# Scores of a gated-linear-attention head: four full-width products replaced by ten 32 by 32 blocks

## What is computed

```python
bcum = jnp.cumsum(lg, axis=3)
q_dec = q * jnp.exp(bcum)
k_intra = k * jnp.exp(-bcum)
causal = jnp.tril(jnp.ones((C, C), bool))
att = jnp.where(causal, jnp.einsum('nbhid,nbhjd->nbhij', q_dec, k_intra), 0.0)
o_intra = jnp.einsum('nbhij,nbhje->nbhie', att, v)
```

## Time and profile before

| what | value |
|---|---|
| median of 3 runs | 1655.56 us (1652.19, 1655.56, 1656.39) |
| profiled execution, span | 1651.1 us |
| time that the page gives around that span | none; the three runs lie 1.1 to 5.3 us above it |
| TensorE busy | 1613.4 us, 98% |
| VectorE, ScalarE, GpSimd busy | 818.7, 458.2, 375.8 us |
| mean granted TensorE clock | 0.99 |

### The profile page before, as it was taken

How to read it: one execution, slowest core, us unless ns; L and a number is a source line. 1 busy time by engine, 2 the same in 40 slices (tenths; PEclk the granted TensorE clock), 3 DMA queues, 4 the chain that set the end, 5 groups by cost and what they waited for, 6 DMA issues and landing times.

```text
span 1651.1 us, 25118 instructions
## 1 busy us (share of the span) xinstructions
PE 1613.4 (98%) x9827; PEld 1501.1 (91%) x9827; DVE 818.7 (50%) x1271; ACT 458.2 (28%) x969; POOL 375.8 (23%) x384
## 2 busy tenths in 40 slices
PE   6999999999999999998999999999999999999996
PEld 5899999999999999998788898888998989979896
DVE  4654449443944475457224562245622356224475
ACT  4321112111211121123325413154040541315423
POOL 3022212211211212211314223133130322314310
PEclk8999999999999999998999999999999999999998
DMA  9512221221122121210202212022120221201312
GB/s 330 193 56 87 62 63 42 84 74 42 55 78 64 57 67 54 77 41 27 64 18 73 84 40 77 13 64 84 53 66 12 64 96 40 77 13 40 110 37 108
DMA packets 137545, 115.03 MB, mean 70 GB/s; under 512 B 6013, under 2 KB 120281, under 8 KB 137442
## 3 DMA queue, kind: packets, MB, share of 16 engines
q1 hardware_dynamic: 135616, 112.87, 22.0%
q10 hardware_dynamic: 1834, 0.74, 0.2%
HBM read 99.05 MB, written 15.00 MB: 69 GB/s over the span
## 4 chain that ended last, share of the span: by engine, by line
PE 94%; DVE 3%; SPq 1%; DMA 1%; ACT 1%; issue 0%; ACTq 0%; DVEq 0%
PE psA L549 40%; PE psB L549 29%; PE psB L1804 8%; PE psA L1804 4%; PE psB L1860 2%; PE psB L1877 2%; PE psX L1842 2%; PE psB L1868 2%; PE psX L1897 1%; DVE a_hi L637 1%; PE psB L1909 1%; PE psX L1720 1%; DMA ada<-in_ada_w 1%; DVE y_rows L1606 0%; PE psB L1910 0%; PE psX L1661 0%
## 5 line engine op out<-in xcount | busy, mean ns | idle before, releaser
L344 POOL TENSOR_TENSOR w_lo<-stage,w_hi 128x1024 fp32r<-128x1024 f32 x100 | 249.7, 2496 | 891.1 <-ACT w_hi L339 891.1
L339 ACT ACTIVATE w_hi<-stage 128x1024 fp32r<-128x1024 f32 x100 | 107.0, 1070 | 433.7 <-PE psB L549 297.6
L549 PE MATMUL psA<-h_hi,w_hi 128*128 128x362 f32 (+1 forms) x864 | 210.9, 349 | 4.1 <-DVE h_lo L453 3.8
L549 PE MATMUL psA<-h_lo,w_hi 128*128 128x362 f32 (+1 forms) x864 | 193.6, 329 | 0.0
L549 PE MATMUL psA<-h_hi,w_lo 128*128 128x362 f32 (+1 forms) x864 | 193.1, 329 | 0.0
L549 PEld LDWEIGHTS psA<-h_hi,w_hi 128*128 128x128 f32 x864 | 151.4, 190 | 27.1 <-issue 21.2
L549 PEld LDWEIGHTS psA<-h_hi,w_lo 128*128 128x128 f32 x864 | 151.5, 190 | 0.0
L549 PEld LDWEIGHTS psA<-h_lo,w_hi 128*128 128x128 f32 x864 | 151.4, 190 | 0.0
L549 PE MATMUL psA<-a_hi,w_hi 128*128 128x362 f32 (+1 forms) x480 | 109.7, 334 | 2.6 <-DVE a_lo L640 1.9
L549 PE MATMUL psB<-h_hi,w_hi 128*128 128x362 f32 (+1 forms) x480 | 109.7, 331 | 0.0
L549 PE MATMUL psB<-h_hi,w_lo 128*128 128x362 f32 (+1 forms) x480 | 107.9, 327 | 0.0
(11 more groups left out here) (345 smaller groups left out, 2790.6 us busy)
## 6 DMA issues: line engine op xcount, KB each, us to landing
stage<-in_gla_w_in SPq DMA_DIRECT2D x40, 512.0 KB, 3.8
stage<-in_pool_w_in SPq DMA_DIRECT2D x32, 512.0 KB, 4.1
ada_stage<-in_ada_w SPq DMA_DIRECT2D x24, 512.0 KB, 3.8
ada<-in_ada_w SPq DMA_DIRECT2D x16, 512.0 KB, 8.4
stage<-in_pool_w_out SPq DMA_DIRECT2D x16, 512.0 KB, 3.4
v<-in_state_gla SPq DMA_DIRECT2D x32, 256.0 KB, 2.6
out_new_gla_sample<-v SPq DMA_DIRECT2D x32, 256.0 KB, 2.1
stage<-in_gla_w_out SPq DMA_DIRECT2D x16, 512.0 KB, 3.7
```

Of the source, the lines that this page charges most:

```text
L339: nc.scalar.activation(slot_hi(plan, j), stage[:, j % 2, :], ACT.Copy).then_inc(lay.hi_done, 1)
L344: nc.gpsimd.tensor_tensor(slot_lo(plan, j), stage[:, j % 2, :], slot_hi(plan, j).bitcast(f32), ALU.subtract).then_inc(lay.lo_done, 1)
L549: last = nc.tensor.matmul(ps[u][:, t, 0:width], weight(w[:, p, :], k), a[:, k, n0:n0 + width], start=(k == 0 and pas == 0), stop=(k == kt ...
```

## The change

`scores` no longer makes one matmul of 128 keys by 32 queries for each query block. It makes ten, each of 32 keys by 32 queries, and each into the 32 partitions of `psX` that belong to its keys, that is into the group of 32 columns of the array with the same number. The order is by distance of key block and query block: first the four with distance 0 (column groups 0, 1, 2, 3), then three with distance 1 (groups 0, 1, 2), two with distance 2 (0, 1), one with distance 3 (group 0). The six blocks that the mask drops are not written; the mask keeps their old content out of `att`. The zeroing of `Kp` and the semaphore `kp_zero` are gone.

```diff
                 wait_apart(pool, L1.unit_done, units(GP, g, GP.unit["LG"] + 1))
-                pool.memset(Kp[:], 0.0).then_inc(kp_zero, 1)
...
                 nc.scalar.activation(ks_s[:], ks_s[:], ACT.Exp).then_inc(smp_exp, 1)
-                act.wait_ge(kp_zero, g + 1)
...
-                    for b in range(4):
-                        last = nc.tensor.matmul(X[0][:, b * CH:(b + 1) * CH], Kp[:, b, :], qd[:, b * CH:(b + 1) * CH],
-                                                start=True, stop=True)
+                    for back in range(4):
+                        for b in range(back, 4):
+                            keys = slice((b - back) * CH, (b - back + 1) * CH)
+                            last = nc.tensor.matmul(X[0][keys, b * CH:(b + 1) * CH], Kp[:, b, keys],
+                                                    qd[:, b * CH:(b + 1) * CH], start=True, stop=True)
                     last.then_inc(att_done, 1)
```

More of the change, by code:

```diff
@@ L286, in trunk @@
         dec_ready = sem("dec_ready")
-        kp_zero, kp_exp, kp_ready = sem("kp_zero"), sem("kp_exp"), sem("kp_ready")
+        kp_exp, kp_ready = sem("kp_exp"), sem("kp_ready")
         qd_arg, qd_exp, qd_ready = sem("qd_arg"), sem("qd_exp"), sem("qd_ready")
```

## The result

The changed kernel takes 1644.40 us in the median of 4 runs (1641.99 to 1645.86) against 1654.99 for the kernel before (1652.19 to 1656.39): ratio 0.9937, 95% interval 0.9923 to 0.9950. That is 10.6 us less where 7.5 were forecast. The profiled spans differ by 9.5 us, 1651.1 to 1641.6.

The account below looks back on a forecast made before the run. TensorE's stream was taken as the bound: 0.25 + 0.03 + 0.22 + 0.12 + 0.11 = 0.73 against 0.97 us per chunk, 7.7 us over 32 chunks, less 0.2 for waits, gives 1648 us. Range 1644.5 to 1655 us.

Parts of the forecast that it names:

- What bounds the kernel: TensorE, busy 98% of the span: the end moves with the length of its own stream.
- TensorE's idle share: Sign: it should rise slightly, since drains show as idle, though the span falls.
- The zeroing is worth nothing: Dropping four `Kp` zeroings of 0.52 us on POOL gains nothing, as ACT's other wait covers them.
- Entry, 0.25: Change from full width to 32-column groups: 0.25 us from last filling matmul to first scores load.
- The body: Ten scores blocks in four column groups side by side: eighth record 0.22 us after the first, 0.031 a round.
- Exit, 0.12: After the last scores matmul, 0.03 us of stream and 0.09 of emptying before the transpose's load.
- the 0.03 for an open first load: The first 32-column scores load lies open for 0.03 us, a quarter of 0.11.
- Then the load of the transpose, 128 columns, lies open for 0.11, which it does not now.: Behind the scores, the transpose's load newly costs 0.11 us per chunk.
- Who must keep up: POOL's last `Kp` slice in chunk 2 is tightest: about 0.09 us left, at most 0.05 charged per head.
- a wait for `Kp` in chunk 2: Sign: if TensorE waits for this buffer there, the prediction is wrong.
- The round that does not halve again: Rival: scores rounds stay near 0.06 us, gain 1.3 us, 1654 us; chance 0.17.
- The case that does not run side by side: Rival: scores records go one after another, 19 steps, 1660 us, or 1677 at 0.06 a step; chance 0.09.

Follow-up runs that it names:

- e1: The changed kernel with the zeroing of `Kp` on GpSimd and ACT's wait for it put back: 1644.56 us, ratio 0.9943 to the kernel before.
- e5: The changed kernel with work left out, one matmul of 32 keys by 32 queries in column group 0 per chunk: 1636.60 us, one run.
- e3: The changed kernel with all 16 blocks of 32 by 32, also those the mask drops, and the zeroing back: 1643.67 us, one run.
- e4: The changed kernel with scores in 64-column halves, six matmuls of 64 keys by 32 queries, zeroing back: 1649.30 us, ratio 0.9977 to the kernel before.
- e2: The changed kernel with the same ten blocks ordered by key block, so that neighbours share a column group: 1645.66 us, one run.
- e7: The changed kernel with the transpose of the keys' rows ahead of the scores instead of behind: 1643.75 us, ratio 0.9938 to the kernel before.
- e6: The changed kernel with work left out, one full-width matmul of 128 keys by 32 queries per chunk, zeroing back: 1634.95 us, one run.
- e8: The changed kernel with the samples' 32-column products moved directly behind the scores at three of four places per head: 1642.48 us, ratio 0.9930.

## Why the prediction came out as it did

*What bounds the kernel.* Right: TensorE's own stream was shortened and the end moved with it. One sign named for it did not come: TensorE's idle share did not rise (1651.1 - 1613.4 = 37.7 us before, 1641.6 - 1604.7 = 36.9 after, 2.28% and 2.25%). The gaps show on the row of the loads instead.

*The zeroing is worth nothing.* Right (e1).

*Entry, 0.25.* Right to the digit, in the trace after and in e5. The Trainium skill's rule in TensorEngine Tiling (Array Packing), Key Properties, that a change of tiling mode drains TensorE, agrees: 28 gaps of 0.23 us, and 0.15 us lost by a lone narrow product against a wide one.

*The body.* Right: 0.24, in the listed window, though the sum had 0.22. The fullest group sets the length (e3), and a round at 64 columns is nearly twice that at 32 (0.058 against 0.032, e4). That the order of the blocks would not matter was nowhere claimed, and it does (e2).

*Exit, 0.12.* Right: the transpose's load came at 0.62 as summed. That this sum is exact is partly luck: the 0.03 for an open first load is not there (the first scores matmul is recorded 0.002 us behind its load), and the body is 0.02 longer than its term.

*"Then the load of the transpose, 128 columns, lies open for 0.11, which it does not now."* This is the step that failed; it is why the gain per chunk was put at 0.24 and not at 0.33. From the last scores matmul to L1860, in the single records of chunk 1, it was 0.255 us before and is 0.293 after, 0.04 more, where the forecast let the tail grow by 0.12 (0.12 + 0.11 in place of 0.11). In the kernel before that load is issued at 857.24 but takes 0.22, where the same load takes 0.139 in the changed kernel and 0.143 in e7. The 0.08 between them is waiting behind the last load of the scores: it too began only when the scores' loads had ended, and lay as open as it does now. The starts say the same. At chunk 1 of the kernel before these are the last three loads of the scores and the load of the transpose:

```profile
862.41 0.41 PEld L1842 LDWEIGHTS psX<-qd,Kp 128*128 128x128 f32 x3
862.66 0.22 PEld L1852 LDWEIGHTS psB<-ident,ks 128*128 128x128 f32 x1
```

Three loads of 0.19 that start 0.11 apart fill the 0.41, so the last starts at 862.63; the next one's turn would be 0.11 later, and the transpose's is recorded 0.03 later, again 0.08 ahead of its turn.

Two like points are the load's real begin, 857.24 + 0.08 = 857.32 before, 0.94 after the last filling matmul at 856.38, against 0.62 now: 0.32 a chunk; or L1860 in both, 0.33. I had set an end that includes the transpose's load (0.73) against one where its matmul was merely issued (0.97). Over 32 chunks the difference is 0.09 x 32 = 2.9 us, the whole of the gap between 7.5 and 10.4. What the runs show is the length of the load and the cost of e7; that the 0.08 is a wait in the queue of loads is read from these lengths and starts and not measured by itself.

*Who must keep up.* Right in place and in the size charged: in chunk 2 of each head the keys' buffer came last, 0.05 us late (at most 0.05 charged). But a wait for `Kp` in chunk 2 stood among the signs that the prediction is wrong, and it came. The working had left 0.09 us of slack with a gain of 0.24; with the 0.33 that TensorE really gained, 0.08 + 0.25 - 0.33 leaves nothing. So this sign follows from the same step, the charge for the transpose's load. e5 and e6 show how near the next bound is: with the chunk made shorter by another 0.2 us it is 0.22 late with an entry to hide under.

*The rivals.* The round that does not halve again is refuted by the 0.24 and by e4. The Trainium skill's rule in TensorE: Matmul & The Clock Gate, Part 3, that a load overlaps a running matmul only when the row group differs, is contradicted with it: all ten blocks use all rows, and 20 loads with 20 matmuls start within 0.24 us. The case that does not run side by side is refuted as well; with a bad order a third of it comes true (e2). One sum in it was off: slower by 0.3%, which is 5 us or 0.156 a chunk, begins at (0.22 + 0.24 + 0.156) / 19 = 0.032 a step and not at 0.034; no chance hangs on it.

## What to carry to other kernels

A group of small products that is bound by its weight loads gains from narrow column groups when the fullest group's rounds, plus one entry and one exit (here 0.24, 0.25 and 0.12 us), are less than the wide loads (0.86); one lone product loses by it, and products that already use column groups should stand next to each other so that they share one change of the array. Order the products so that neighbours fall in different groups. When two versions of a stretch are compared, take the same event in both, and take it behind the stretch: the record of a load starts when it is issued, and its length can show that it then stood in a queue (here 0.22 us against 0.14).

## What was not expected of the hardware

Sixteen blocks cost almost as much as ten (0.26 against 0.24 us). The order of the same ten blocks changes them from 0.24 to 0.36 us. In e8 products of a later line started ahead of earlier ones that wait for another column group. The load ahead of a 32-bit transpose is shorter than others of its width: 0.139 against 0.19 us.
